# Dense product in native fp32 on 1104 columns, one-hots moved between ScalarE and VectorE, two dot pairs a unit on TensorE, top-k woven between dots

## The chip, the cores and the metric

The kernel runs on one core of one Trainium2 chip. Its time is the device time of one execution in microseconds (us). Three executions of the kernel before took 2683.0 to 2688.03 us, with a median of 2685.36 us.

## The reference, cut to what matters

One decoder layer on 272 tokens (16 meta, 256 real) of width 2048: a layer norm, two token mixers that read one input projection, a second layer norm, then a feed-forward part (PEER) that gathers experts, and a third norm. The change lies in the PEER part, for the 256 real tokens (two tiles of 128):

```
q = (t @ peer_wq).reshape(T, PEER_HEADS, 2, HALF_KEY)
sc = einsum('thpk,hpnk->thpn', q, peer_keys)
s_top, i_top = top_k(sc, 16)
cand = s_top[..., 0, :, None] + s_top[..., 1, None, :]
best_s, best_pos = top_k(cand, 16)           # 16 experts of 128*128 per token and head
g = softmax(best_s)
a = gelu(einsum('td,tkd->tk', xb, peer_u[eb]))
out = einsum('tk,tkd->td', g * a, peer_v[eb])  # 8 heads * 16 experts
```

Each token uses 128 of 16384 rows of peer_u and as many of peer_v, all 2048 wide, in fp32.

## The kernel before, in words

**Stages.** First the input projection and the mixers: weights stream in in 48 groups through SyncE's DMA queue, ScalarE and VectorE split each into two fp32r parts, TensorE multiplies. Then the **dots**, the **placement** and the **product**, which the change touches.

**Dots.** A unit is one head of one tile: 16 units (PH = 8 heads, 2 tiles), units 0 to 7 for tile 0 and 8 to 15 for tile 1. For a unit, `topk` on VectorE (17 chained steps) finds the 16 experts of each of 128 tokens, GpSimd issues 16 indirect DMAs (`gather_u`, L1852), each of which brings one row of peer_u per token (128 x 8 KB) into a ring of 8 buffers, and 16 dot products follow. VectorE makes most of them (`dot`, L1625, one instruction of 2048 columns each). From unit 2 on, the six rows of `PAIRS` (0,1), (5,6), (10,11) go to TensorE (`dots_pair`): it transposes the two rows block by block into PSUM (L817), ScalarE copies each of 8 blocks to `ut` (L908, `pair_copies`), TensorE multiplies with the transposed tokens (L430), and VectorE reads the diagonal (`pair_dots`, L1636). A buffer is free once its dot or its last transpose is done; GpSimd's queue waits for that in row order, so a row that is late holds back all gathers behind it. `gelu` and `softmax_exp` on ScalarE and `coefs` on VectorE give the weights.

**Placement.** The output is not summed from 256 gathered peer_v rows over all 2048 columns. For the first FD columns the kernel builds, per tile, a matrix of 128 tokens x 16384 experts that holds the weights (`wt0`, `wt1`): for each token, the product of two one-hot matrices (`oh`, 128 slots x 128 keys, one scaled by the weight). `one_hots` (L1654, L1655) makes them on VectorE in a ring of 5, `place` multiplies them on TensorE, `w_copy` moves four tokens at a time to SBUF on ScalarE. Tile 0 is placed during units 8 to 15, 16 tokens a unit, in pieces ahead of each `pair_dots` (`WTOK` = 6, 5, 5); tile 1 is placed after the last dot.

**Product.** 128 panels (128 experts x FD = 1344 columns of peer_v, 5376 B a row) stream in through SyncE's queue into 4 buffers. ScalarE and VectorE split each into an fp32r high and low part (`v_hi_of`, `v_lo_of`), and the matching piece of `wt` too (`w_hi_of`, `w_lo_of`). TensorE makes three fp32r products (high*high, high*low, low*high) for two tiles in three column cuts, 18 matmuls a panel, accumulated in six PSUM banks. The other 704 columns (2816 B a row) are gathered per slot (`gather_v`, L1863, ring of 4) and added by VectorE (`add_row`, L1681), 256 rows of 128 tokens. VectorE's order in this stage is add, split, add, split of `wt`. A last layer norm writes the output.

The order on each engine is written out by hand, and engines meet only at semaphores.

## Time and profile before

| | |
|---|---|
| median of 3 executions | 2685.36 us |
| the profiled execution | 2681.95 us |
| its span | 2680.1 us |
| busy: PE, DVE, ACT, POOL | 86%, 65%, 39%, 27% |
| granted TensorE clock, mean | 0.944 |
| HBM read | 655.69 MB, 245 GB/s over the span |

The page divides the span into 40 slices of 67 us. In slices 20 to 23 (1340 to 1608 us) the DMA share reads 9 (90% or more) and the rate is 380 to 395 GB/s; in the next six it reads 7 with 279 to 325 GB/s; slice 31 has 25 GB/s; after that it reads 8 or 9 with 284 to 323 GB/s. PE is TensorE, DVE VectorE, ACT ScalarE, POOL GpSimd, PEld TensorE's weight load.

### The profile page before, as it was taken

Reading aid. Unit: us, or ns where it says so; the run is one execution under the profiler, and the core shown is the slowest. Engines: PE = TensorE matmul, PEld = TensorE weight load, DVE = VectorE, ACT = ScalarE, POOL = GpSimd, SP = SyncE. Lnnn points to the kernel's source line nnn. Section 1 sums busy time; section 2 is a strip of 40 time slices with the busy share of each in tenths; the row PEclk is TensorE's granted clock in tenths of the full one; section 3 lists DMA queues with packets and bytes.
Section 4 is the critical chain, followed back from the end, with each engine's and each line's share of the span. In section 5 each row is a group of like instructions: output and inputs, shape, how many; then the busy total and the mean of one; then the engine's idle time right before and its main releaser. Section 6 shows DMA issues by size and latency. Waiting matters only on the chain.

```text
span 2680.1 us, 36941 instructions
## 1 busy us (share of the span) xinstructions
PE 2305.8 (86%) x13296; PEld 1992.0 (74%) x13296; DVE 1750.9 (65%) x2931; ACT 1035.3 (39%) x1481; POOL 717.5 (27%) x558
## 2 busy tenths in 40 slices
PE   7999999999999999993588877676778988888885
PEld 5888999988899888793466666565666777776774
DVE  5344455554455555578877777776759788878777
ACT  4444433444444444641233333333333333333331
POOL 0000000000000000023655533333330566556664
PEclk9999999999999999997798988888898999999997
DMA  6444555555555555395999987777760899889986
GB/s 174 115 140 141 172 177 185 185 177 192 193 177 190 188 188 177 109 371 230 395 383 393 380 324 304 306 307 279 311 258 25 284 314 323 309 307 316 311 314 221
DMA packets 217084, 659.68 MB, mean 246 GB/s; under 512 B 18784, under 2 KB 68064, under 8 KB 183520
## 3 DMA queue, kind: packets, MB, share of 16 engines
q0 software_dynamic: 57488, 361.79, 35.7%
q1 hardware_dynamic: 159456, 296.05, 33.2%
q8 instruction: 84, 1.38, 0.2%
q14 instruction: 56, 0.46, 0.0%
HBM read 655.69 MB, written 2.10 MB: 245 GB/s over the span
## 4 chain that ended last, share of the span: by engine, by line
PE 54%; DMA 20%; DVE 12%; issue 9%; ACT 2%; POOL 1%; DVEq 0%; POOLq 0%; SPq 0%; ACTq 0%
PE ps L430 50%; DMA v_rows<-in_v_gathered,idx_all 12%; DMA u_rows<-in_peer_u,idx_all 6%; DVE h L1681 3%; PE ps L817 3%; DVE junk L1625 2%; DMA v_raw<-in_peer_v 1%; DMA raw<-in_peer_wq 1%; POOL u_rows L1852 1%; ACT L908 0%; DVE lo L1289 0%; ACT hi L908 0%; POOL v_rows L1863 0%; PE ps L515 0%; ACT ut L908 0%
## 5 line engine op out<-in xcount | busy, mean ns | idle before, releaser
L1289 DVE TENSOR_TENSOR lo<-raw,hi 128x1024 fp32r<-128x1024 f32 x368 | 448.5, 1225 | 492.2 <-ACT hi L908 491.2
L908 ACT ACTIVATE hi<-raw 128x1024 fp32r<-128x1024 f32 x376 | 397.4, 1060 | 571.7 <-PE ps L430 560.1
L1852 POOL DMA_INDIRECT u_rows<-in_peer_u,idx_all x256 | 343.1, 1340 | 516.8 <-PE ps L817 335.8
L1625 DVE SCALAR_TENSOR_TENSOR junk<-u_rows,h 128x2048 bf16<-128x2048 f32 x172 | 388.6, 2288 | 122.0 <-DMA u_rows<-in_peer_u,idx_all 121.8
L430 PE MATMUL ps<-v_hi,w_hl 128*128 128x512 f32 (+1 forms) x1536 | 384.1, 379 | 77.2 <-DVE w_hl L1669 64.6
L430 PE MATMUL ps<-xh,hi 128*128 128x256 f32 (+2 forms) x1536 | 440.6, 287 | 2.5 <-ACT qkv L908 1.3
L1863 POOL DMA_INDIRECT v_rows<-in_v_gathered,idx_all x256 | 351.8, 1374 | 324.3 <-DVE h L1681 275.5
L430 PE MATMUL ps<-xh,lo 128*128 128x256 f32 (+2 forms) x1536 | 435.6, 284 | 0.0
L430 PE MATMUL ps<-xl,hi 128*128 128x256 f32 (+2 forms) x1536 | 434.9, 283 | 0.0
L430 PEld LDWEIGHTS ps<-v_hi,w_hl 128*128 128x128 f32 x1536 | 274.6, 194 | 144.9 <-issue 82.9
L430 PE MATMUL ps<-ut,h1t 128*128 128x256 f32 x1344 | 361.3, 398 | 19.4 <-ACT ut L908 19.3
L1681 DVE SCALAR_TENSOR_TENSOR h<-v_rows,coef_all,h 128x704 f32<-128x704 f32 x256 | 243.0, 949 | 116.5 <-DMA v_rows<-in_v_gathered,idx_all 114.4
L908 ACT ACTIVATE v_hi<-v_raw 128x1344 fp32r<-128x1344 f32 x128 | 170.1, 1329 | 366.1 <-DMA v_raw<-in_peer_v 324.3
L908 ACT ACTIVATE ut<-ps 128x512 f32<-128x512 f32 x336 | 197.3, 596 | 277.7 <-PE ps L817 277.7
L817 PE MATMUL ps<-ident,u_rows 128*128 128x128 f32 x1344 | 215.5, 293 | 101.4 <-DMA u_rows<-in_peer_u,idx_all 59.6
L430 PEld LDWEIGHTS ps<-xh,hi 128*128 128x128 f32 x1536 | 290.4, 189 | 12.3 <-issue 8.6
L430 PEld LDWEIGHTS ps<-xl,hi 128*128 128x128 f32 x1536 | 290.9, 189 | 0.0
L430 PEld LDWEIGHTS ps<-xh,lo 128*128 128x128 f32 x1536 | 290.1, 189 | 0.0
L817 PEld LDWEIGHTS ps<-ident,u_rows 128*128 128x128 f32 x1344 | 182.1, 153 | 135.1 <-issue 109.6
L430 PEld LDWEIGHTS ps<-ut,h1t 128*128 128x128 f32 x1344 | 237.9, 198 | 58.9 <-ACT ut L908 39.5
L1795 POOL TENSOR_TENSOR rstd<-rstd,m_half 128x1 f32<-128x1 f32 (+1 forms) x7 | 5.5, 786 | 816.0 <-DVE rstd L1530 800.4
L1663 DVE TENSOR_TENSOR v_lo<-v_raw,v_hi 128x1344 fp32r<-128x1344 f32 x128 | 198.6, 1552 | 17.2 <-ACT v_hi L908 17.2
(230 smaller groups left out, 3099.3 us busy)
## 6 DMA issues: line engine op xcount, KB each, us to landing
raw<-in_w_in SPq DMA_DIRECT2D x96, 1024.0 KB, 5.1
v_raw<-in_peer_v SPq DMA_DIRECT2D x128, 672.0 KB, 6.5
raw<-in_w_in SPq DMA_DIRECT2D x64, 256.0 KB, 3.1
raw<-in_w_in SPq DMA_DIRECT2D x32, 512.0 KB, 4.7
...
```

Source lines behind the costliest of these rows:

```text
L430: return nc.tensor.matmul(o, a, b, start=start, stop=stop)
L817: last = nc.tensor.transpose(ps[:, 3 + g % 2, (2 * n + r) * P:(2 * n + r + 1) * P], u_rows[k % RING][:, kt * P:(kt + 1) * P], ident[:, :])
L908: return nc.scalar.activation(o, i, f, **kw)
L1289: V.tensor_tensor(raw_lo[:, hh // 2, k4, :] if kept else lo[:, hh % SLOT_N, :, :], raw[:, hh // 2, k4, :], (kept_hi(hh) if kept else hi[:, ...
L1625: V.scalar_tensor_tensor(junk[:, n % 2, :], u_rows[k % (RING if u else HEAD_RING)][:, :], 1.0, h1[:, u // PH, :], ALU.mult, ALU.mult, accu ...
L1663: V.tensor_tensor(v_lo[i % RAWS][:, :], v_raw[i % RAWS][:, :], v_hi[i % HIS][:, :].bitcast(F32), ALU.subtract).then_inc(S("vlo_ready"), 1)
L1681: V.scalar_tensor_tensor(h1[:, T, FD:D], v_rows[n % VRING][:, :], coef_all[:, T, s:s + 1], h1[:, T, FD:D], ALU.mult, ALU.add).then_inc(S(" ...
L1795: Q.tensor_tensor(rstd[:cnt, n:n + 1], rstd[:cnt, n:n + 1], m_half[:cnt, 0:1], ALU.pow).then_inc(S(name + "_rstd"), 1)
L1852: Q.indirect_dma_start(u_rows[slot][:, :], None, peer_u, bass.IndirectOffsetOnAxis(ap=idx_all[:, n:n + 1], axis=0)).then_inc(u_in[slot], 16)
L1863: Q.indirect_dma_start(v_rows[n % VRING][:, :], None, v_gathered, bass.IndirectOffsetOnAxis(ap=idx_all[:, n:n + 1], axis=0)).then_inc(v_in ...
```

## The change

It changes five things (in the diff, the first `one_hots` is ScalarE's for tile 0, the second VectorE's for tile 1).

1. **Product.** FD is 1104, in three cuts of 368 columns. The panels (4416 B a row) and `wt` are multiplied as they are, in fp32, without the split: 6 matmuls a panel. The gathered part grows to 944 columns (3776 B a row). Five panel buffers in place of four, a ring of seven rows in place of four.
2. **Dots.** Two pairs a unit on TensorE, rows (0,1) and (8,9), so 12 dots a unit on VectorE in place of 10.
3. **Top-k.** A dot is put behind nearly each of the chained steps of `topk(u+2)`; before, the whole of `topk(u+2)` stood behind the dots of unit u. It reads the scores in place. `topk(1)` moves ahead of the dots of unit 0, between the splits of weight groups, and GpSimd's wait for the end of the projections moves behind the first four gathers of unit 1.
4. **Placement of tile 0.** The one-hots are made on ScalarE by Square, Relu(1 - x) and Copy with a scale, in chunks of four tokens (ring of 3 chunks), two chunks after each pair's copies; TensorE places a chunk half a unit later, behind the next pair.
5. **Placement of tile 1.** Still on VectorE after the last dot, in chunks: the key one-hots of four tokens by one instruction of 512 columns, every fourth chunk's key one-hots on ScalarE. The transpose of the slots stands ahead of `tile_open`.

```diff
-PAIRS = ((0, 1), (5, 6), (10, 11))
+PAIRS = ((0, 1), (8, 9))
-FD = 1344
+FD = 1104
+CW = 368
-RAWS, HIS, WBUFS = 4, 3, 2
-VRING = 4
+RAWS = 5
+VRING = 7
...
             def panel(i):
-                pe.wait_ge(S("vhi_ready"), i + 1)
-                pe.wait_ge(S("vlo_ready"), i + 1)
...
+                pe.wait_ge(vr_in[i % RAWS], 16 * (i // RAWS + 1))
                 for T in range(NT):
-                    for wn, v in ((0, v_hi[i % HIS]), (0, v_lo[i % RAWS]), (1, v_hi[i % HIS])):
-                        for n, (a, b) in enumerate(CUTS):
...
+                    for n, (a, b) in enumerate(CUTS):
+                        last = mm(ps[:, 3 * T + n, 0:CW], wt_rows(T, i, 1)[:, 0, :], v_raw[i % RAWS][:, a:b], False,
+                                  i == NKEY - 1)
...
+            def place(c):
+                bank = 6 + (c + 1) % 2
+                if c < CHUNKS_T:
+                    pe.wait_ge(S("oh_ready"), c + 1)
+                else:
+                    pe.wait_ge(S("oh_dve_ready"), c - CHUNKS_T + 1)
...
+            def one_hots(c):
+                if c >= OHR:
+                    act.wait_ge(S("w_done"), c - OHR + 1)
+                o = oh[c % OHR]
+                t0 = c % CHUNKS_T * WB
+                for q in range(WB):
+                    for n in range(2):
+                        ins = A(o[:, n, q, :], iota[:, :], ACT.Square, scale=-1.0, bias=slots_t[:, 1 + n, t0 + q:t0 + q + 1])
+                ins.then_inc(S("one_hot_squares"), 1)
+                act.wait_ge(S("one_hot_squares"), c + 1)
+                A(o[:, :, :, :], o[:, :, :, :], ACT.Relu, scale=-1.0, bias=one[:, 0:1]).then_inc(S("one_hot_units"), 1)
+                act.wait_ge(S("one_hot_units"), c + 1)
+                for q in range(WB):
+                    ins = A(o[:, 0, q, :], o[:, 0, q, :], ACT.Copy, scale=slots_t[:, 0, t0 + q:t0 + q + 1])
+                ins.then_inc(S("oh_ready"), 1)
...
                     pair_copies(u, pair)
+                    if pair == 0:
+                        gelu(u - 1)
+                        if u + 1 < 2 * PH:
+                            softmax_exp(u + 1)
                     if u >= PH:
+                        half = placed_half(u, pair)
+                        if half >= 0:
+                            for c in range(2):
+                                one_hots(2 * half + c)
+                        if half >= 1:
+                            for c in range(2):
+                                w_copy(2 * (half - 1) + c)
+            for c in range(2 * (2 * PH - 1), CHUNKS_T):
+                one_hots(c)
+            gelu(2 * PH - 1)
...
+            def one_hots(c):
+                dve.wait_ge(S("w_done"), c - OHR + 1)
...
+                if c % 4 != ACT_B:
+                    V.tensor_tensor(o[:, 1, :, :], iota[:, :].unsqueeze(1).to_broadcast([P, WB, P]),
+                                    slots_t[:, 2, t0:t0 + WB].unsqueeze(2).to_broadcast([P, WB, P]), ALU.is_equal)
+                for q in range(WB):
+                    ins = V.tensor_scalar(o[:, 0, q, :], iota[:, :], slots_t[:, 1, t0 + q:t0 + q + 1],
+                                          slots_t[:, 0, t0 + q:t0 + q + 1], ALU.is_equal, ALU.mult)
...
+            topk(1, scores_of(1), {4 * n - 10: lambda n=n: split_lo(G_WQ + 1, n) for n in range(AHEAD, 2 * AHEAD)})
...
+                    topk(u + 2, scores_of(u + 2), {n + 1: lambda n=n: unit_part(u, n) for n in range(min(parts, 15))})
...
-            for i in range(NKEY):
-                add_row(2 * i)
-                if i + 3 < NKEY:
-                    v_lo_of(i + 3)
-                add_row(2 * i + 1)
...
+            for n in range(NT * SLOTS):
+                add_row(n)
```

SyncE's first panel waits for the last top-k, the second and third for the last pair, the others for the last dot. GpSimd's `gather_v` waits for `tile_opened` at row 3 and for the last placement at row 5.

VectorE in unit 8, the first of tile 1, behind its first three dots. Before, one pair of `one_hots` per token stood ahead of the diagonal of a pair:

```order
L1625 SCALAR_TENSOR_TENSOR junk,dots<-u_rows_92,h_84 128x2048
L1659 TENSOR_SCALAR h_84<-h_84 128x704
L1654 TENSOR_SCALAR ohs<-iota,slots_t 128x128
L1655 TENSOR_SCALAR ohs<-iota,slots_t 128x128
...
L1636 SCALAR_TENSOR_TENSOR junk_148,dots<-ps,ident 128x128 x2
L1625 SCALAR_TENSOR_TENSOR junk,dots<-u_rows_95,h_84 128x2048
```

Now, in a later unit of tile 1 (unit 13), the steps of the top-k stand between dots, and no one-hot is left in a unit:

```order
L1582 MAX kv<-sc_all 128x8 x2
L1632 SCALAR_TENSOR_TENSOR junk,dots<-u_rows_90,h_84 128x2048
L1585 MAX_INDEX ki<-kv,sc_all 128x8
L1586 MATCH_REPLACE scw<-kv,sc_all 128x128
L1585 MAX_INDEX ki<-kv,sc_all 128x8
L1586 MATCH_REPLACE scw<-kv,sc_all 128x128
L1632 SCALAR_TENSOR_TENSOR junk,dots<-u_rows_91,h_84 128x2048
L1589 MAX kv<-scw 128x8 x2
L1632 SCALAR_TENSOR_TENSOR junk,dots<-u_rows_92,h_84 128x2048
```

The one-hots left VectorE's units, and each chained step now has a dot behind it.

ScalarE in tile 1 (`ut` is a pair's block, `wt` the placed weights). Before, a placed chunk was copied behind the copies of each pair:

```order
L908 ACTIVATE ut<-ps 128x512 x8
L908 ACTIVATE wt_103<-ps 128x128x4
L908 ACT_TABLE_LOAD
L908 ACTIVATE exps,exp_sums<-best,nbest 128x16
L908 ACTIVATE ut<-ps 128x512 x8
```

Now, first half of a unit:

```order
L904 ACTIVATE ut<-ps 128x512 x8
L904 ACT_TABLE_LOAD
L904 ACTIVATE gel<-dots 128x16
L904 ACT_TABLE_LOAD
L904 ACTIVATE exps,exp_sums<-best,nbest 128x16
L904 ACTIVATE ohs_101<-iota,slots_t 128x128 x8
L904 ACTIVATE ohs_101<-ohs_101,one 128x1024
L904 ACTIVATE ohs_101<-ohs_101,slots_t 128x128 x4
L904 ACTIVATE ohs_102<-iota,slots_t 128x128 x8
L904 ACTIVATE ohs_102<-ohs_102,one 128x1024
L904 ACTIVATE ohs_102<-ohs_102,slots_t 128x128 x4
L904 ACTIVATE wt_105<-ps 128x128x4 x2
```

26 one-hot instructions were put between a pair's copies and the next pair's; no table load stands among them.

TensorE in the product, one panel (`v_raw` is the panel as loaded), now:

```order
L428 MATMUL ps<-v_raw_109,wt_105 128x368 x3
L428 MATMUL ps<-v_raw_109,wt_0_106 128x368 x3
```

Six matmuls stand where 18 stood, and nothing of ScalarE or VectorE is ahead of them.

## Rows read from the trace of the kernel before

**Rows 1.** Windows by stage: us; PE, PEld, DVE, ACT, POOL busy; PEclk, DMA share, GB/s

```profile
1275.00:1539.00 264.00, 202.00 (x1088) 167.84 (x1088) 205.29 (x430) 98.54 (x169) 147.84 (x97) 0.89 0.97 387
1539.00:1980.00 441.00, 324.01 (x1775) 278.32 (x1775) 309.95 (x775) 152.75 (x259) 152.93 (x128) 0.87 0.78 306
2075.00:2660.00 585.00, 505.80 (x2304) 413.29 (x2304) 458.23 (x508) 204.52 (x251) 345.23 (x252) 0.97 0.88 305
```

**Rows 2.** Timeline of POOL: first gathers of units 1, 2, 8, and the last of unit 15

```profile
1244.45 0.94 POOL L1852 DMA_INDIRECT u_rows<-in_peer_u,idx_all  x1 [25.26 <-DVE idx_all L1614]
...
1275.60 1.91 POOL L1852 DMA_INDIRECT u_rows<-in_peer_u,idx_all  x1 [0.30 <-issue]
...
1539.24 0.94 POOL L1852 DMA_INDIRECT u_rows<-in_peer_u,idx_all  x1 [0.30 <-issue]
...
1979.62 0.93 POOL L1852 DMA_INDIRECT u_rows<-in_peer_u,idx_all  x1 [0.30 <-issue]
```

**Rows 3.** Groups by line and form from 1539 to 1980 us

```profile
L430 PE MATMUL ps<-ut,h1t 128*128 128x256 f32 x768 | 202.8, 392 | 16.8 <-ACT ut L908 16.8
L1625 DVE SCALAR_TENSOR_TENSOR junk<-u_rows,h 128x2048 bf16<-128x2048 f32 x80 | 180.5, 2288 | 70.1 <-DMA u_rows<-in_peer_u,idx_all 70.1
L1852 POOL DMA_INDIRECT u_rows<-in_peer_u,idx_all x128 | 153.5, 1199 | 288.1 <-PE ps L817 244.4 <-issue 43.4 <-DVE junk L1636 0.3
...
L430 PE MATMUL ps<-ohs 128*128 128x128 f32 x236 | 50.9, 383 | 91.5 <-DVE ohs L1655 91.4
```

**Rows 4.** Timeline of DVE: first and last of one top-k, its start and the dot behind

```profile
1421.80 0.29 DVE L1573 COPY sc<-sc_all 128x256 f32<-128x256 f32 x1
...
1433.33 2.29 DVE L1625 SCALAR_TENSOR_TENSOR junk<-u_rows,h 128x2048 bf16<-128x2048 f32 x1
```

**Rows 5.** Timeline of PE and ACT: a burst after a wait, one without, a pair's copies

```profile
1651.20 2.60 PE L430 MATMUL ps<-ohs 128*128 128x128 f32 x10 [8.58 <-DVE ohs L1655]
...
1665.08 1.28 PE L430 MATMUL ps<-ohs 128*128 128x128 f32 x10
...
1668.43 1.07 ACT L908 ACTIVATE ut<-ps 128x512 f32<-128x512 f32 x2
...
1677.17 0.60 ACT L908 ACTIVATE ut<-ps 128x512 f32<-128x512 f32 x1 [0.70 <-PE ps L817]
```

**Rows 6.** Groups of ACT by form, whole span

```profile
L908 ACT ACTIVATE hi<-raw 128x1024 fp32r<-128x1024 f32 x376 | 397.4, 1060 | 571.7 <-PE ps L430 560.1 <-DMA raw<-in_peer_wq 11.4
...
L908 ACT ACT_TABLE_LOAD x39 | 50.0, 1283 | 1.5 <-PEq L1892 0.8
...
L908 ACT ACTIVATE h<-ps,par 128x128 f32<-128x128 f32 x32 | 11.7, 467 | 0.1
...
L908 ACT ACTIVATE wt<-ps 128x128 f32<-128x128 f32 x32 | 8.7, 273 | 0.0
```

**Rows 7.** Timeline: last weights, first and last one-hot of tile 1, first panel

```profile
2002.62 0.23 DVE L1644 SCALAR_TENSOR_TENSOR coef_all<-gel,exp_scale,exps 128x16 f32<-128x16 f32 x1 [1.14 <-ACT gel L908]
...
2011.13 0.28 DVE L1654 TENSOR_SCALAR ohs<-iota,slots_t 128x128 f32<-128x128 f32 x1
...
2072.44 0.34 DVE L1655 TENSOR_SCALAR ohs<-iota,slots_t 128x128 f32<-128x128 f32 x1
...
2075.47 1.46 PE L430 MATMUL ps<-v_hi,w_hl 128*128 128x512 f32 x3 [2.15 <-ACT w_hl L908]
```

**Rows 8.** VectorE's tensor-tensor by form: 1024 columns (page), 256 columns (1539 to 1980 us)

```profile
L1289 DVE TENSOR_TENSOR lo<-raw,hi 128x1024 fp32r<-128x1024 f32 x368 | 448.5, 1225 | 492.2 <-ACT hi L908 491.2
...
L1604 DVE TENSOR_TENSOR oh_k<-pos2f,iota 128x256 f32<-128x256 f32 x14 | 5.3, 421 | 1.0
```

**Rows 9.** Product: `add_row` (2075 to 2660 us); timeline of PE at two panels' starts

```profile
L1681 DVE SCALAR_TENSOR_TENSOR h<-v_rows,coef_all,h 128x704 f32<-128x704 f32 x256 | 243.0, 949 | 116.5 <-DMA v_rows<-in_v_gathered,idx_all 114.4
...
2083.75 1.40 PE L430 MATMUL ps<-v_hi,w_hl 128*128 128x512 f32 x6
...
2087.47 1.40 PE L430 MATMUL ps<-v_hi,w_hl 128*128 128x512 f32 x6
```

274 lines of the change are left out of this document (115 added, 159 removed).

## The prediction

> **What bounds the kernel now.** I read the windows by stage first, then GpSimd's gathers in order of time, then the groups and the timelines of each stage.
>
> In the dots of tile 0 the DMA engines are the bound: share 0.97 at 387 GB/s, with 264 us from the first gather of unit 2 to that of unit 8 [rows 1, 2], (1539.24 - 1275.60) / 6 = 43.9 us a unit. In tile 1 the same 16 rows a unit take (1979.62 - 1539.24) / 8 = 55.0 us [rows 2] at a share of 0.78 [rows 1]. GpSimd waits there 244.4 us for a pair's last transpose, TensorE 91.4 us for VectorE's one-hots and VectorE 70.1 us for rows [rows 3]: a ring, in which one-hots on VectorE delay TensorE, which frees buffers late, which delays the rows that VectorE waits for. From the last weights to the first panel lie 2075.47 - 2002.62 = 72.9 us [rows 7]: VectorE makes one-hots. In the product the share is 0.88 at 305 GB/s for 585 us, with TensorE busy for 506 [rows 1]. It is nearly DMA-bound, with gaps in which neither queue has a row to move.
>
> **The change, part by part.** The sum is made against the profiled execution, 2681.95 us, which is 3.4 us under the median of the runs.
>
> *Start of the dots.* GpSimd sat 25.3 us before unit 1's first gather, for the top-k of unit 1 [rows 2]. That top-k now stands ahead of unit 0's dots. What comes next is late for VectorE: 16 dots of unit 1 and a top-k of 1433.33 - 1421.80 = 11.5 us [rows 4], 16 x 2.2 + 11.5 = 47 us, more than the 43.9 us that the rows need. So not 25 us are gained but what VectorE saves, and that is its own waits. Between 0 and 25 I take 10: the first rows are there early, but VectorE must still work off unit 1.
>
> *Tile 0, units 2 to 7.* VectorE gets two dots more and loses one pair's diagonals. In tile 1 it was busy 309.95 us in 8 units [rows 1], 38.7 each, of which 16 tokens of one-hots are 16 x 0.46 = 7.3 (from the run of 128: (2072.78 - 2011.13 - 3.1 for two splits) / 128 [rows 7]). The rest, 31.4, plus 2 x 2.29 [rows 3] is 36 us, and with the pauses of the chain at most 40, under 43.9. TensorE goes from three pairs to two. Rows 0, 1, 8 and 9 now all use the same two buffers: a pair holds them some 11 us, and new rows need about 8.5, so 19.5 to 21.5 against half a unit of 22. It fits barely, and I charge 0.3 us a unit, **+2** (between -3 and +15). The cover is the five rows that still stand in the ring; if a pair takes 2 us more it is gone, 6 x 4 = +24.
>
> *Tile 1, units 8 to 15.* VectorE is now as in tile 0. ScalarE takes the one-hots. Its costs: 8 blocks of a pair take 1677.77 - 1668.43 = 9.3 us once it is free [rows 5]. A small activation of 128 columns is 0.27 us without a per-partition operand, 0.47 with two, about 0.10 of it overlapped (11.7 us for 32) [rows 6]; I take 0.27 for one such operand. A chunk: 12 x 0.27 + 1.06 for 1024 columns + 0.3 for its two waits = 4.6 us. Half a unit: 9.3 + 2 x 4.6 + 2 x 0.55 for the copies of placed chunks = 19.6; once a unit, 2 x 1.28 for tables [rows 6] + 0.7 for gelu and exp; 42.5 us and two handovers of 0.5, **43.5 us**, the same as the DMA's 43.9. Nothing of it lies on VectorE's path. Three chains of 40 to 43.9 us that meet twice a unit don't run at the longest of them; I take 45.5 us: 8 x 45.5 = 364 against 440.4, **-76**. Bounds: 43.9 gives -89; with 0.37 for a small activation the chain is 48.5 and gives -52. On the engine choice, one token's one-hots cost 0.46 us on VectorE and 4.6 / 4 = 1.15 on ScalarE, worked out above. The Trainium skill, ScalarE: Activation LUTs, section Rules for kernel authors, says that relu and simple arithmetic belong on VectorE; by that rule, the work would be 2.5 times as long here and the placement would gain nothing. The rows say that ScalarE was busy 152.75 of 441 us [rows 1], so the longer work has room; the rule would put tile 1 at its present 440 us and the sum at 2649.
>
> *Last rows to last weights*, 23.0 us [rows 2, 7]: the last pair ends earlier in the unit, but two more chunks (9.2 us) stand ahead of the last gelu on ScalarE. **+2** (-3 to +12).
>
> *Tile 1's placement.* Before, 72.9 us. Now VectorE's chunk of four tokens: 512 columns of tensor-tensor, between 0.42 (256) and 1.23 (1024) [rows 8], by their slope 0.69, some 0.60 in a stream, and 4 x 0.26; 24 such chunks and 8 without the first: 24 x 1.64 + 8 x 1.04 = 48 us. TensorE: a matmul leaves two records, 8 records a chunk at 0.128 (10 in 1.28) [rows 5] are 1.0 us, hidden. Lead-in and last copy 9 us: 57, **-16** (-25 to 0).
>
> *Product.* TensorE: before, a panel of 18 took 2087.47 - 2083.75 = 3.72 us [rows 9]. Now 6 fp32 matmuls of 368 columns. `ut` x `h1t` is fp32 with 256 columns, two records each: 202.8 us busy for 384 matmuls [rows 3] is 0.53 us at a mean clock of 0.87 [rows 1], 0.46 at the full one, so 368 columns take 0.66 us and a panel 4.0: 128 x 4.0 = 508 us, a floor below what follows. VectorE: 256 adds of 944 columns at 949 + 240 x 1.04 = 1.20 us [rows 9] = 307 us, its splits gone. ScalarE nothing. DMA: before, 128 x 128 x 5376 + 256 x 128 x 2816 B = 180.4 MB, now 128 x 128 x 4416 + 256 x 128 x 3776 = 196.1 MB, less 5.2 MB that are in their buffers when the stage begins (5 panels, 5 rows). The rate is the term that no row shows. At this stage's 305 / 0.88 = 347 GB/s per full share and tile 0's share of 0.97 [rows 1], 336 GB/s and 568 us; at the unchanged 305 GB/s 626; at tile 0's 387 GB/s 493. I take 336: nothing holds the queues back any more (seven rows, add and product no longer in step), as in tile 0's ring, but rows stay of the size of this stage, about 4 KB against 8. With 7 us for start and last add 575: **-10** (-85 to +48). Layer norm and output have the same columns: 0.
>
> Sum: 2681.95 - 10 + 2 - 76 + 2 - 16 - 10 = 2574; with the median in mind **2575**.
>
> **The rivals.**
>
> *The product keeps its DMA rate* (0.15). For: no more than 0.88 was seen with two queues at once, and each row may cost more than its bytes. 190.9 MB at 305 GB/s + 7 = 633 us, +48, total 2575 + 58 = **2633** with no gain there. The Trainium skill, DMA: Bandwidth & Descriptors, section How a descriptor splits into AXI transactions, speaks for it: transfers go in pieces of 256 B from aligned addresses; 5376 and 2816 are multiples of 256, 4416 and 3776 aren't, and by my estimate from that page a gathered row costs 121 beats where its bytes make 118, 2.5% more. No row here shows an unaligned transfer. By that alone the product would take 14 us more, 2589. Against: ring depth was what stopped the gathers (add_row waited 114.4 us for rows [rows 9]).
>
> *ScalarE or the two shared buffers bound the units* (0.15). Units of 49 us in tile 1, 45.5 in tile 0: +28 + 8, **2611**. For: 43.5 is a sum of estimates, and a pair after a wait starts slow. Against: with three pairs tile 0 was at 0.97.
>
> *The product goes at tile 0's rate* (0.10): 493 us are under TensorE's 508, so 508 + 7 = 515 and **2515**. For: gathered rows of 3776 B are longer. Against: TensorE would then have to run without a gap.
>
> *Slower: TensorE's clock falls in the product* (0.05). It would wait 0.4 us in each panel of 4.4, and its granted clock is 2.4 GHz or half. Ten placement records took 2.60 us after a wait of 8.58 and 1.28 without [rows 5]. At half clock a panel is 8.0 us, all 128 make 1024 and the total **3024**. The point from which it decides: the total passes 2682 when the stage takes 682 us, 5.3 a panel, with a third of the columns at half clock. Against: the clock was 0.97 with TensorE idle 14% [rows 1], and now it would be 4.0 of 4.4, idle 10%.
>
> *The change doesn't take the one-hots off the path*: if ring and semaphores let TensorE wait for ScalarE as it did for VectorE, that is the second rival at its worst, 55 us a unit, 2651, inside its chance.
>
> **How the numbers follow.** The forecast, 2575, has 0.55. Together with the first two rivals it spans 2535 to 2633. The range reaches from **2525** to **2640** and leaves out the fast product and the slow clock, less than 2 in 10. Faster by more than 0.2% (5 us, about what a measurement of this kernel can tell from none): all but the slow clock and a pile-up of the bad ends, **0.95**; the same 0.01; slower 0.04.
>
> **What would show it.** GpSimd's first gathers of two units 44 us apart in tile 0 and 45 to 46 in tile 1, with a DMA share from 0.90 up; a ScalarE chunk of 4.6 us; under 60 us from the last weights to the first panel; in the product a share of 0.95 or more, a TensorE clock over 0.95, panels of 3.7 to 4.0 us with waits for `v_raw`. It is wrong if tile 1 stays above 50 us a unit, if the product takes over 600, or if TensorE, not the DMA, ends last there.

## The result and the profile after

| | before | after |
|---|---|---|
| median | 2686.49 us (4 runs) | 2497.56 us (4 runs) |
| ratio, with its 95% interval | | 0.9297 [0.9281, 0.9313] |
| the profiled execution | 2681.95 us | 2497.36 us |
| its span | 2680.1 us | 2495.5 us |
| HBM read | 655.69 MB | 671.42 MB |

The change makes the kernel 7.0% faster. The forecast was 2575 us, and the result lies 27 us under the lower end of its range, 2525. The two profiled executions differ by 184.6 us. Read against the marks that the prediction uses, the parts are:

| part | before | after | difference | predicted |
|---|---|---|---|---|
| first gather of unit 2 | 1275.60 | 1270.08 | -5.5 | -10 |
| tile 0, units 2 to 7 | 263.6 | 267.0 | +3.4 | +2 |
| tile 1, first to last gather | 440.4 | 370.6 | -69.8 | -76 |
| last gather to last weights | 23.0 | 31.7 | +8.7 | +2 |
| last weights to first panel | 72.9 | 58.8 | -14.1 | -16 |
| product, first panel to the end of the last | 584.5 | 477.2 | -107.4 | -10 |
| layer norm and output | 20 | 20 | 0 | 0 |

Six of seven terms came out within 7 us. The product alone brought ten times what was forecast for it.

The page of the changed kernel, its slices of 62 us. PEclk is TensorE's granted clock and DMA the share, both in tenths:

```profile
PEclk9999999999999999999967777777878899999998
DMA  5444465555565555547999999889998099999997
GB/s 163 130 143 143 135 193 179 185 182 188 185 196 183 186 188 190 172 149 255 354 357 366 376 385 381 347 347 356 353 375 331 17 374 411 412 411 411 409 410 294
```

The windows by stage of the changed kernel, with the columns of [rows 1]: tile 0, tile 1, product.

```profile
1270.00:1537.00 267.00, 155.42 (x765) 129.28 (x765) 226.44 (x432) 76.41 (x126) 178.54 (x96) 0.76 0.97 379
1537.00:1908.00 371.00, 230.45 (x1182) 196.14 (x1182) 271.59 (x494) 240.11 (x548) 191.49 (x128) 0.78 0.90 353
1998.00:2475.00 477.00, 474.98 (x1536) 291.65 (x1536) 304.58 (x255) 0.19 (x1) 383.99 (x251) 1.00 1.01 405
```

Against [rows 1]: tile 0 is as it was, tile 1 went from a share of 0.78 to 0.90, and the product from 305 to 405 GB/s. Six slices in a row (374 us) stand at 409 to 412 GB/s. TensorE is busy there for 474.98 of 477.00 us, so it is a bound. The DMA was expected to be the only one.

The groups of the same stage (1998 to 2475 us) say what each engine waited for (a group of matmuls has two records for each matmul):

```profile
L428 PE MATMUL ps<-v_raw,wt 128*128 128x368 f32 x1536 | 475.4, 472 | 2.6 <-DMA v_raw<-in_peer_v 1.8 <-ACT wt L904 0.8
L1859 POOL DMA_INDIRECT v_rows<-in_v_gathered,idx_all x251 | 384.0, 1530 | 129.0 <-issue 79.6 <-PE ps L428 43.5 <-DVE h L1680 5.9
L1680 DVE SCALAR_TENSOR_TENSOR h<-v_rows,coef_all,h 128x944 f32<-128x944 f32 x255 | 306.5, 1202 | 172.5 <-DMA v_rows<-in_v_gathered,idx_all 171.6
```

TensorE waits 1.8 us for panels in the whole stage. GpSimd, which issues the gathers, waits 5.9 us for a free row buffer. In 128 panels, 475.4 / 128 = 3.71 us each, a matmul of 368 columns is 0.62 us. VectorE waits 171.6 us for rows, and only the 5.9 us of GpSimd are waits for VectorE. The 18 fp32r matmuls of a panel before took 3.72 us [rows 9]: native fp32 on fewer columns made TensorE's panel no shorter, it took the splits away.

The end of the stage has a second chain that ends with TensorE's. The last matmuls and the last five adds of rows, from the timeline of 2455 to 2495.5 us:

```profile
2454.55 20.88 PE L428 MATMUL ps<-v_raw,wt 128*128 128x368 f32 x67
2469.60 6.46 DVE L1680 SCALAR_TENSOR_TENSOR h<-v_rows,coef_all,h 128x944 f32<-128x944 f32 x5 [0.81 <-DMA v_rows<-in_v_gathered,idx_all]
```

The matmuls end at 2475.43 and the adds at 2476.06. GpSimd's gathers stand back to back in this stage, 1.53 us and some 0.3 of issue each. So the stage is bound twice, by TensorE's matmuls and by the stream of gathered rows, and shortening one of them alone would gain almost nothing.

Tile 1 after the change, ScalarE's timeline through one unit (1730.05 to 1777.67 us):

```profile
1730.05 2.43 ACT L904 ACTIVATE ohs<-iota,slots_t 128x128 f32<-128x128 f32 x8
1732.51 1.15 ACT L904 ACTIVATE ohs<-ohs,one 128x1024 f32<-128x1024 f32 x1
1733.69 1.28 ACT L904 ACTIVATE ohs<-ohs,slots_t 128x128 f32<-128x128 f32 x4
1734.88 2.43 ACT L904 ACTIVATE ohs<-iota,slots_t 128x128 f32<-128x128 f32 x8
...
1739.70 1.05 ACT L904 ACTIVATE wt<-ps 128x512 f32<-128x512 f32 x2
1740.88 0.60 ACT L904 ACTIVATE ut<-ps 128x512 f32<-128x512 f32 x1
...
1751.21 0.60 ACT L904 ACTIVATE ut<-ps 128x512 f32<-128x512 f32 x1 [0.71 <-PE ps L815]
1751.83 1.28 ACT L904 ACT_TABLE_LOAD   x1
...
1754.96 2.43 ACT L904 ACTIVATE ohs<-iota,slots_t 128x128 f32<-128x128 f32 x8
...
1777.67 2.44 ACT L904 ACTIVATE ohs<-iota,slots_t 128x128 f32<-128x128 f32 x8
```

A chunk (the one-hots of four tokens) is 1734.88 - 1730.05 = 4.83 us, of which 2.43 are eight squares, 0.30 each. The eight copies of a pair take 1740.88 to 1751.81, 10.9 us, and in the other half 1765.56 to 1777.78, 12.2. Between them the engine has no idle time except the pair's own waits for transposes. The unit is 1777.67 - 1730.05 = 47.6 us, and the first gathers of units 9 and 15 are (1873.65 - 1588.82) / 6 = 47.5 us a unit apart (before, (1931.94 - 1590.93) / 6 = 56.8): the chain on ScalarE is the pace of tile 1.

The end of tile 1, ScalarE and VectorE of the changed kernel:

```profile
1918.90 2.43 ACT L904 ACTIVATE ohs<-iota,slots_t 128x128 f32<-128x128 f32 x8
...
1939.16 0.20 ACT L904 ACTIVATE gel<-dots 128x16 f32<-128x16 f32 x1
1939.39 0.23 DVE L1651 SCALAR_TENSOR_TENSOR coef_all<-gel,exp_scale,exps 128x16 f32<-128x16 f32 x1 [14.05 <-ACT gel L904]
```

After the last pair, four chunks stand ahead of the last gelu, 1939.16 - 1918.90 = 20.3 us. The last weights wait for it.

### The profile page after: what moved, and what is told of

It is laid out like the page before. It is cut to its first block, busy times and chain, and to the rows that moved or that the text cites. A ratio compares the mean times of both kernels' runs of the same rounds, so it can differ in the third digit from the quotient of the medians.

```text
span 2495.5 us, 32610 instructions
## 1 busy us (share of the span) xinstructions
PE 2122.0 (85%) x11632; PEld 1746.1 (70%) x11632; DVE 1571.4 (63%) x2299; ACT 927.9 (37%) x1571; POOL 837.0 (34%) x559
## 3 DMA queue, kind: packets, MB, share of 16 engines
HBM read 671.42 MB, written 2.10 MB: 270 GB/s over the span
## 4 chain that ended last, share of the span: by engine, by line
PE 58%; issue 15%; POOL 9%; DMA 7%; ACT 6%; DVE 5%; DVEq 0%; POOLq 0%; ACTq 0%
PE ps L428 52%; POOL v_rows L1859 7%; DMA u_rows<-in_peer_u,idx_all 6%; PE ps L815 5%; ACT ohs L904 3%; DMA v_rows<-in_v_gathered,idx_all 1%; POOL u_rows L1846 1%; DVE ohs L1665 1%; ACT L904 1%; DVE ohs L1662 0%; DVE lo L1296 0%; ACT hi L904 0%; PE ps L513 0%; ACT wt L904 0%; DVE h L1680 0%
## 5 line engine op out<-in xcount | busy, mean ns | idle before, releaser
L1846 POOL DMA_INDIRECT u_rows<-in_peer_u,idx_all x256 | 421.7, 1647 | 365.8 <-PE ps L815 199.7
L1632 DVE SCALAR_TENSOR_TENSOR junk<-u_rows,h 128x2048 bf16<-128x2048 f32 x200 | 458.2, 2292 | 136.8 <-DMA u_rows<-in_peer_u,idx_all 107.2
L428 PE MATMUL ps<-v_raw,wt 128*128 128x368 f32 x1536 | 475.4, 472 | 2.6 <-DMA v_raw<-in_peer_v 1.8
L428 PEld LDWEIGHTS ps<-v_raw,wt 128*128 128x128 f32 x1536 | 291.7, 190 | 186.0 <-DMA v_raw<-in_peer_v 2.6
L1680 DVE SCALAR_TENSOR_TENSOR h<-v_rows,coef_all,h 128x944 f32<-128x944 f32 x256 | 307.7, 1202 | 172.5 <-DMA v_rows<-in_v_gathered,idx_all 171.6
L428 PE MATMUL ps<-ut,h1t 128*128 128x256 f32 x896 | 267.7, 432 | 11.5 <-ACT ut L904 11.5
L904 ACT ACTIVATE ut<-ps 128x512 f32<-128x512 f32 x224 | 132.9, 597 | 343.2 <-PE ps L815 343.1
L428 PEld LDWEIGHTS ps<-ut,h1t 128*128 128x128 f32 x896 | 175.1, 218 | 42.3 <-ACT ut L904 25.5
L428 PE MATMUL ps<-hi,xh 128*128 128x512 f32 x256 | 101.7, 397 | 1.8 <-DVE t_y L1452 1.3
L428 PE MATMUL ps<-lo,xh 128*128 128x512 f32 x256 | 100.6, 393 | 0.0
```

The lines of the kernel that those rows point to most:

```text
L428: return nc.tensor.matmul(o, a, b, start=start, stop=stop)
L904: return nc.scalar.activation(o, i, f, **kw)
L1632: V.scalar_tensor_tensor(junk[:, n % 2, :], u_rows[k % (RING if u else HEAD_RING)][:, :], 1.0, h1[:, u // PH, :], ALU.mult, ALU.mult, accu ...
L1680: V.scalar_tensor_tensor(h1[:, T, FD:D], v_rows[n % VRING][:, :], coef_all[:, T, s:s + 1], h1[:, T, FD:D], ALU.mult, ALU.add).then_inc(S(" ...
L1846: Q.indirect_dma_start(u_rows[slot][:, :], None, peer_u, bass.IndirectOffsetOnAxis(ap=idx_all[:, n:n + 1], axis=0)).then_inc(u_in[slot], 16)
```

## The experiments

Two things needed an explanation: why the product's rate rose by a third, and what it was in the edits that shortened tile 1's middle units from 56.8 to 47.5 us. The first theory for the product was that the DMA engines carry more per unit of share when VectorE and ScalarE leave the splits out of their buffers' way (contention). The rivals were the rows' ring, from four to seven buffers, and the number of columns. For tile 1 the theory was ScalarE's chain, and the rivals were the half unit of delay and the third pair that TensorE lost. Each run is given by its ratio to the kernel before, measured beside it. That kernel's own median was between 2679.80 and 2686.49 us in these groups of runs, so two kernels of different groups that are less than 10 us apart are better compared by their ratios than by their medians.

### The product: what set its rate

**The columns alone**, in the kernel before:

```diff
-FD = 1344
+FD = 1104
+CW = 368
-CUTS = ((0, 512), (512, 1024), (1024, FD))
+CUTS = ((0, 368), (368, 736), (736, FD))
...
```

> The kernel before with only the column split changed to 1104 in three cuts of 368: panels still split into fp32r parts by ScalarE and VectorE, 18 matmuls a panel, rings of four. Theory A (the splits, not the columns, held the product back): VectorE's step for a panel is two adds of 1.20 us, one split of 1104 columns (about 1.3 us) and half of two splits of the weights (0.4), 4.1 us against 4.1 before, in step with rings of four; the DMA moves 1.53 MB a panel in place of 1.41, at the old 305 to 315 GB/s 4.9 us a panel, so the product takes 610 to 640 us and the kernel 2700 to 2740. Rival B (the columns did it): the product falls clearly under 585 us, toward 480 to 520, the kernel under 2620.

Measured: 2701.51 us, ratio 1.0094 [1.0066, 1.0122], so 0.9% longer. The product ran at 323 to 332 GB/s in the slices, where the kernel before has 307 to 323; the stage took 594 us, under the 610 to 640 expected. More columns on the row side raise the rate by a few per cent, far from 411 GB/s, and in sum they cost 22 us.

**More work on the engines that the change relieved**, in the changed kernel: a ScalarE copy of 1344 columns per panel in one run, a VectorE tensor-tensor of 768 columns per panel in the other. Nothing reads their output.

```diff
+            for i in range(NKEY):
+                act.wait_ge(S("panel_done"), i + 1)
...
+                A(scratch[:, :], wt0[:, 100:111, :].rearrange("p a b -> p (a b)")[:, 0:1344], ACT.Copy
+                  ).then_inc(S("scratch_done"), 1)
```

```diff
                 add_row(n)
+                if n % 2 == 0 and n:
...
+                    V.tensor_tensor(scratch[:, 0:768], wt0[:, 100:106, :].rearrange("p a b -> p (a b)"),
+                                    wt0[:, 106:112, :].rearrange("p a b -> p (a b)"), ALU.subtract
+                                    ).then_inc(S("scratch_done"), 1)
```

> The changed kernel, with one extra ScalarE copy of 128 x 1344 fp32 from one place of SBUF to another per panel, for which nobody waits: ScalarE's traffic of the kernel before, without its dependences. Theory D (ScalarE's traffic beside them stretches DMA packets, which took 20 to 25% more than their usual time before and 2% more now): DMA rate falls from 411 to some 350 GB/s, the product takes 540 to 570 us, kernel 2560 to 2590. Rival A (only dependences and order held the queues back): within 5 us of the changed kernel's 2497.6.

> The changed kernel, with one extra VectorE tensor-tensor of 128 x 768 fp32 per panel between the adds, for which nobody waits: about half of VectorE's splits of the kernel before. VectorE then needs 2 x 1.20 + 0.95 = 3.4 us a panel, under TensorE's 3.72. Theory D2 (VectorE's traffic stretches DMA packets or GpSimd's issues): product 510 us or more, kernel 2530 or more. Rival A (only order and dependences): under 10 us more than 2497.6.

Measured: 2498.31 us, ratio 0.9335 [0.9309, 0.9361], and 2503.57 us, 0.9347 [0.9325, 0.9369]. Windows of 2100 to 2400 us, first with the copies, then with the tensor-tensors:

```profile
2100.00:2400.00 300.00, 300.00 (x972) 184.30 (x970) 192.88 (x161) 107.23 (x81) 246.31 (x160) 1.00 1.02 411
```

```profile
2100.00:2400.00 300.00, 300.00 (x972) 184.31 (x971) 255.69 (x241) 0.00 (x0) 247.66 (x160) 1.00 1.02 411
```

ScalarE busy for 107 us, or VectorE for 256 instead of 193, and the rate stays at 411 GB/s. The contention theory falls for each load by itself: taking either off its engine was not what made transfers faster. Both loads at once, and VectorE's whole load of before, were not run. By their ratios the two kernels take 0.4% and 0.5% more than the change, and for the second the intervals don't overlap; its profiled execution is 4.0 us longer, and its last weights are already 4.0 us late (1943.40 for 1939.39), ahead of the first added instruction.

**Both rings as before, then each alone:**

```diff
-RAWS = 5
-VRING = 7
+RAWS = 4
+VRING = 4
```

> The changed kernel with four panel buffers and four row buffers in place of five and seven. Theory A (the splits held the queues back, not the rings): a row has 1.86 us, a slot of four 7.4 us, and its cycle is issue 1.3, transfer and landing about 4 to 5, add 1.2: about 7, so the product goes from 477 to 480 to 500 us, kernel 2500 to 2520. Rival C (ring depth was what stopped the gathers before): the product goes back to 550 us or more, kernel 2570 or more.

> The changed kernel with the ring of gathered rows at four, panel buffers at five as changed. Theory C (too few gathers in flight cost the DMA engines their rate; the four-and-four kernel took 88 us more): all of that loss is here, product about 565 us, kernel 2575 to 2595. Rival C2 (the panel buffers share it): 2530 to 2560.

> The changed kernel with four panel buffers, the ring of rows at seven as changed. Theory C: nothing, within 5 us of 2497.6, since TensorE waits for a panel only 2 us in all. Rival C2: 20 us or more above it.

| panels | rows | median | ratio |
|---|---|---|---|
| 4 | 4 | 2585.53 us | 0.9646 [0.9622, 0.9669] |
| 5 | 4 | 2586.28 us | 0.9626 [0.9608, 0.9643] |
| 4 | 7 | 2503.69 us | 0.9319 [0.9303, 0.9335] |
| 5 | 7 | 2497.56 us | 0.9297 [0.9281, 0.9313] |

With four row buffers 88 us of the gain are gone: theory C, and not A's 2500 to 2520. The fifth panel buffer is worth some 6 us, where theory C said 5 at most, and the intervals overlap. This is where most of the product's 107 us came from: three more buffers for the gathered rows. The rest is small: with four of them, the changed kernel's product takes 2570.18 - 1998.55 = 571.6 us against the 584.5 of before.

Windows with four row buffers (five panels), while TensorE has panels and after its last:

```profile
2000.00:2475.00 475.00, 473.94 (x1533) 290.70 (x1531) 244.64 (x204) 0.00 (x0) 249.28 (x205) 1.00 0.97 359
```

```profile
2475.00:2570.00 95.00, 0.02 (x1) 0.00 (x0) 59.38 (x50) 0.00 (x0) 61.92 (x47) 0.52 0.78 244
```

TensorE does its 128 panels in 475 us here too. In that time VectorE adds 204 of the 256 rows, 475 / 204 = 2.33 us each, and the rest takes 95 us with TensorE idle. Without panels beside them, the same four buffers bring 50 rows in these 95 us, 1.90 each: a buffer's turn (from one gather into it to the next) falls from 9.3 to 7.6 us, so it isn't a constant of the ring. In these 475 us the share is 0.97. A reader of that number alone would call it DMA-bound, as I read tile 0's; but the same 475 us carry 407 GB/s in the changed kernel, with more buffers.

**How many row buffers:**

> The changed kernel with five row buffers in the product (four gave 2586, seven 2498). Theory A (each buffer is busy 9.3 us a turn, whatever their number: 4 x 2.33 us a row in the run with four): a row each 9.3 / 5 = 1.86 us, which is TensorE's own pace of 3.72 / 2, so five buffers already nearly reach the full rate: 2498 to 2506 us and 405 GB/s or more. Theory B (more transfers in flight share the queues, and a buffer's turn grows to 10 us or more, as 4 x 2.26 became 5 x 2.01 in the kernel before): a row each 2.0 us, 256 rows in 515 us: about 2535 us, and 385 GB/s.

> Six row buffers. Theory A: as with seven, 2495 to 2502 us. Theory B: a turn of 10.5 to 11 us over six is 1.8 us a row, under TensorE's 1.86, so here too the time of seven: 2496 to 2506 us. A third, that each buffer is worth the same down to seven: (2586 - 2498) / 3 = 29 us each, so 2527.

Windows of 2100 to 2400 us with four, five and six row buffers (three kernels; the changed one has 411 GB/s there):

```profile
2100.00:2400.00 300.00, 300.00 (x972) 184.35 (x971) 154.94 (x129) 0.00 (x0) 163.50 (x129) 1.00 0.97 359
```

```profile
2100.00:2400.00 300.00, 300.00 (x972) 184.39 (x971) 179.14 (x149) 0.00 (x0) 211.37 (x150) 1.00 1.01 393
```

```profile
2100.00:2400.00 300.00, 300.00 (x972) 184.52 (x971) 190.71 (x159) 0.00 (x0) 248.28 (x159) 1.00 1.02 408
```

| row buffers | us per row | buffer's turn | median | ratio |
|---|---|---|---|---|
| 4 | 300 / 129 = 2.33 | 9.3 us | 2586.28 us | 0.9626 [0.9608, 0.9643] |
| 5 | 300 / 150 = 2.00 | 10.0 us | 2519.52 us | 0.9389 [0.9363, 0.9415] |
| 6 | 300 / 159 = 1.89 | 11.3 us | 2499.36 us | 0.9329 [0.9307, 0.9350] |
| 7 | 300 / 160 = 1.88 | 13.1 us | 2497.56 us | 0.9297 [0.9281, 0.9313] |

Beside panels, a buffer's turn (gather, landing, add) is 9 to 10 us when the ring is the limit, and longer where it isn't. From six buffers on a row takes 1.88 us, and GpSimd waits at most 0.3 us of these 300 for a buffer: the ring is no longer the limit. Against 1.88, a turn of 10.0 us wants 10.0 / 1.88 = 5.3 buffers, so five are short, six are enough, and the seventh buys at most a few us.

What holds a row at 1.88 us is not TensorE, though its half panel takes nearly the same, 3.71 / 2 = 1.86: in the changed kernel neither a gather nor an `add_row` waits for a matmul. The run with 1344 columns on TensorE, told below, has rows of 2816 B that come faster than half a panel of 2.25 us. It gathers its last row at 2362.51, some 210 us before its last matmul ends. While rows come, its rate is nearly that of the change (window of 2010 to 2360 us):

```profile
2010.00:2360.00 350.00, 350.00 (x933) 176.96 (x932) 226.53 (x238) 0.00 (x0) 271.39 (x239) 1.00 1.01 398
```

A row takes 350 / 238 = 1.47 us there. A gather's time on GpSimd is no fixed price either. With four, five and seven row buffers it is 1.27 us at 359 GB/s, 1.42 at 393 and 1.55 at 411 (2100 to 2400 us), with rows of 2816 B 1.14 at 398, and the shortest take 0.94. Queues that are full near 400 to 411 GB/s would look like this; no run separates the DMA engines from GpSimd's issuing. So the changed product meets two limits at once, and that they lie within 1 us of each other is luck.

For five, theory A (a fixed turn) said 2498 to 2506 and theory B 2535: the measured 2519.52 lies between, since the turn grew from 9.3 to 10.0 us. For six, both said about what was measured, and "each buffer is worth the same" (2527) is out.

**One more row buffer in the kernel before:**

```diff
-VRING = 4
+VRING = 5
```

> The kernel before with a ring of five gathered rows in place of four, nothing else changed. Theory C (ring depth held its product at 305 GB/s): a row's cycle of 8.9 us over five slots is 1.8 us, so its product is bound next by VectorE's 3.9 to 4.1 us a panel and falls from 585 to 525 to 545, kernel 2635 to 2645. Rival A (VectorE's and ScalarE's splits in step with the adds held it): within 10 us of the kernel before.

Measured: 2625.76 us, ratio 0.9777 [0.9760, 0.9793]. One buffer gives 60 us, with splits and columns as they were, 9 us better than the range of theory C, and its product takes 525 us. Waits of 2100 to 2400 us (engine, line, what it waited for: us in total, times, longest), of the kernel before:

```profile
POOL v_rows L1863 <- DVE h L1681: 108.8, 99, 3.2
DVE h L1681 <- DMA v_rows<-in_v_gathered,idx_all: 58.4, 53, 2.5
```

with five row buffers:

```profile
POOL v_rows L1865 <- DVE h L1681: 58.5, 86, 2.6
DVE h L1681 <- DMA v_rows<-in_v_gathered,idx_all: 29.0, 43, 1.9
```

and of the changed kernel:

```profile
DVE h L1680 <- DMA v_rows<-in_v_gathered,idx_all: 108.0, 161, 1.1
POOL v_rows L1859 <- DVE h L1680: 0.3, 1, 0.3
```

In the kernel before, both sides of the row ring waited for each other, GpSimd for a buffer that VectorE had to free and VectorE for the row. VectorE's order also bound the two halves of the product together: `add_row(2i)`, the split of a panel, `add_row(2i + 1)`. So a panel could not go faster than two rows, and 585 us / 256 = 2.29 us a row, 9.1 a turn, was the pace of everything. The change cut that tie and deepened the ring; now the wait for a buffer is 0.3 us. Cutting the tie alone left a row at 2.33 us, as the run with four row buffers shows. Whether the splits would have let the kernel before reach the same time with six or seven is open: no run has them there, and at five its TensorE is already busy for 280.56 of 300 us.

**TensorE as a new bound**, the changed kernel with 1344 columns on TensorE again (buffers are moved to make room, and the third and fifth panels wait longer):

```diff
-FD = 1104
-CW = 368
+FD = 1344
...
+CW = 448
...
```

> The changed kernel with the old column split: 1344 columns in three cuts of 448 in native fp32, 704 gathered, rings of five and seven. TensorE is the bound: 6 x 448 columns at 1.69 ns (0.62 us for 368) are 4.53 us a panel, 128 of them 580 us against 475; kernel 2595 to 2605, with the DMA share near 0.85 and 311 GB/s. Rival (something else than TensorE would pace it, as in the kernel before): above 2620.

Measured: 2597.94 us, ratio 0.9676 [0.9658, 0.9694], 100 us over the change. The time is as expected; the share is not: it was to be near 0.85, and is 1.01 while the rows come, since they run ahead. Group of 2100 to 2400 us:

```profile
L430 PE MATMUL ps<-v_raw,wt 128*128 128x448 f32 x800 | 300.8, 539 | 0.0
```

800 records are 400 matmuls, 0.75 us each, against 0.62 for 368 columns (972 records in 300 us): both some 1.68 ns a column at a granted clock of 1.00, which is four cycles of 2.4 GHz. 128 panels of 4.5 us are 576 us. So 1104 columns are no detail: with native fp32, TensorE's time goes with the columns, and the split between TensorE and the rows is what the change had to shift.

### Tile 1: what set the unit

**Less work on ScalarE.** This kernel leaves out the Relu and three of four Copies of each chunk, so tile 0's weights are not placed rightly; it only shows what their time is worth:

```diff
-                A(o[:, :, :, :], o[:, :, :, :], ACT.Relu, scale=-1.0, bias=one[:, 0:1]).then_inc(S("one_hot_units"), 1)
-                act.wait_ge(S("one_hot_units"), c + 1)
-                for q in range(WB):
-                    ins = A(o[:, 0, q, :], o[:, 0, q, :], ACT.Copy, scale=slots_t[:, 0, t0 + q:t0 + q + 1])
-                ins.then_inc(S("oh_ready"), 1)
+                A(o[:, 0, 0, :], o[:, 0, 0, :], ACT.Copy, scale=slots_t[:, 0, t0:t0 + 1]).then_inc(S("oh_ready"), 1)
```

> The changed kernel, whose ScalarE makes only the Squares of tile 0's one-hots and one small Copy a chunk; Relu and three Copies a chunk are left out, so the weights of tile 0 are not placed rightly. Theory E (ScalarE's chain of copies and one-hots, 47.6 us a unit back to back, is what paces tile 1): 2.1 us less a chunk, 8.5 us a unit, so the units fall from 47.7 to the DMA's 44 and the last gelu comes 4 us earlier; with three chunks' worth less behind the last pair 2497.6 falls by 26 to 35, to 2463 to 2472. Rival F (the two buffers that both pairs share pace the units): they stay at 46.5 or more, kernel above 2485.

Measured: 2474.35 us, ratio 0.9234 [0.9210, 0.9258]. The gathers of units 9 to 15 are 44.3 us apart on average ((1855.97 - 1590.08) / 6), where they were 47.5. ScalarE's length was the pace, as theory E has it, and under it lies the 44 us of tile 0. The total is 2 us over the range that this theory gave.

**The one-hots of tile 0 on VectorE**, all of them, a half, and the last two chunks only. Everything else stays as in the change, with the placing half a unit later:

```diff
...
                 elif n == 6:
                     pair_dots(u, 0)
+                    tile0_chunks(u, 0)
                 elif n == 13:
                     pair_dots(u, 1)
+                    tile0_chunks(u, 1)
...
```

> The changed kernel with tile 0's one-hots made on VectorE in chunks of four tokens (one instruction for the keys, four for the scaled ones, 1.63 us a chunk) behind each pair's diagonal, still placed half a unit later. If only the move to ScalarE gained in tile 1, the units go back toward 55 us (kernel 2550 or more). Theory E: VectorE has 34 us of work a unit and gets 6.5 more, 40.5 plus its pauses, ScalarE falls to 30: units of 44 to 45.5 and a last gelu right behind the last pair, 2465 to 2485, faster than with ScalarE.

> The changed kernel with every odd chunk of tile 0 and chunk 30 on VectorE, the other even ones on ScalarE. ScalarE 9.6 us less a unit, 38, VectorE 3.3 more, 37: no engine near the DMA's 44 us, so the units are DMA-bound: 44.3 against 47.7, 7.5 x 3.4 = 25 and 9 at the end: 2460 to 2470, the fastest of these. Rival: the shared buffers hold the units at 46 or more, 2478 or more.

> The changed kernel with only the last two of tile 0's 32 chunks on VectorE, which waits there 14 us for the last gelu. Two chunks of 4.8 us go from ScalarE's path between the last pair and the last gelu: 8 to 10 us less, 2488 to 2490. Rival: TensorE or the copies of placed chunks are next, 3 us or less gained.

| on VectorE | median | ratio |
|---|---|---|
| chunks 0 to 31 | 2471.52 us | 0.9212 [0.9186, 0.9238] |
| every other, and chunk 30 | 2469.89 us | 0.9212 [0.9189, 0.9235] |
| chunks 30 and 31 | 2488.31 us | 0.9277 [0.9256, 0.9298] |
| none (the change) | 2497.56 us | 0.9297 [0.9281, 0.9313] |

Both upper rows beat the change, by 26 and 28 us. Windows of 1589 to 1812 us, of the change and with all chunks on VectorE:

```profile
1589.00:1812.00 223.00, 141.76 (x731) 121.00 (x730) 168.22 (x334) 159.50 (x370) 118.36 (x78) 0.79 0.90 354
```

```profile
1589.00:1812.00 223.00, 146.21 (x781) 125.68 (x780) 203.62 (x441) 72.74 (x122) 138.04 (x80) 0.80 0.96 369
```

VectorE is busy 203.62 of 223 us and still not in the way: the units are (1860.13 - 1588.72) / 6 = 45.2 us apart and the DMA share is 0.96. So moving the one-hots to ScalarE didn't bring the gain of tile 1; it cost a part of it. The last two chunks alone bring 9 us by the medians and 5 by the ratios, whose intervals overlap. In the profile the last gelu starts 1932.24 - 1921.63 = 10.6 us after the last pair, where it was 20.3.

**Without the half unit of delay**: TensorE places a chunk right behind the pair in whose half it is made. One run with the one-hots on VectorE, one with them on ScalarE:

```diff
-                    if u >= PH and placed_half(u, pair) >= 1:
+                    if u >= PH and placed_half(u, pair) >= 0:
                         for c in range(2):
-                            place(2 * (placed_half(u, pair) - 1) + c)
-            for c in range(2 * (2 * PH - 2), CHUNKS_T):
+                            place(2 * placed_half(u, pair) + c)
+            for c in range(2 * (2 * PH - 1), CHUNKS_T):
```

> One-hots of tile 0 on VectorE as in the run that took 2471.5 us, but TensorE places them in the half unit in which they are made, right behind the pair, as the kernel before did. Theory A (the half unit of delay is what took the one-hots off the path): TensorE waits in each half for the pair's diagonals and 3.6 us of one-hots, 4 to 5 us, twice a unit, and the units of tile 1 grow from 44.7 to 48 to 53 us: total 2500 to 2540. Theory B (the delay is worth little; the third pair and VectorE's load were what made 55 us): TensorE is idle 77 us of 223 in these units, the wait falls into that, and units stay at 45 to 46: total 2468 to 2482, a few us of it from a shorter end of tile 1.

> The changed kernel with its one-hots on ScalarE, but placed in the half unit in which they are made. ScalarE makes the two chunks behind the pair's copies, in 9.7 us, and TensorE waits for them before it turns the next pair. Theory A (without the delay the one-hots on ScalarE are a chain in series with TensorE): a half unit is a pair of 11 us, two chunks of 9.7, the placing and the next wait; units from 47.6 to 52 or more, total 2530 to 2580. Theory B (ScalarE's own chain of 47.6 us sets the pace in either order): 2490 to 2505.

| one-hots on | placed | median | ratio | unit |
|---|---|---|---|---|
| VectorE | half a unit later | 2471.52 us | 0.9212 [0.9186, 0.9238] | 45.2 us |
| VectorE | at once | 2492.97 us | 0.9293 [0.9271, 0.9316] | 48.7 us |
| ScalarE | half a unit later | 2497.56 us | 0.9297 [0.9281, 0.9313] | 47.5 us |
| ScalarE | at once | 2527.66 us | 0.9435 [0.9411, 0.9459] | 51.0 us |

TensorE's row in the groups of 1589 to 1812 us, one-hots on VectorE, with the delay and without it:

```profile
L436 PE MATMUL ps<-ohs 128*128 128x128 f32 x144 | 17.5, 275 | 0.0
```

```profile
L436 PE MATMUL ps<-ohs 128*128 128x128 f32 x144 | 34.1, 432 | 81.9 <-DVE ohs L1679 81.9
```

The delay takes 81.9 us of waits in five units out of TensorE's way, and with them the slow start: the same 144 records take 17.5 us after other work and 34.1 after a wait. It is worth 3.5 us a unit with the one-hots on either engine. With them on VectorE theory B had expected nothing and A 3 to 8, and the total, 2492.97, lies between their ranges. With them on ScalarE both ranges were missed as well: A said 52 us a unit or more and 2530 to 2580, against 51.0 and 2527.66. But 48.7 is still 8.1 us under the 56.8 of before. That remainder belongs to what both runs share with the change: two pairs in place of three, one-hots in chunks behind the pair's diagonals and no longer ahead of them, and the top-k between the dots. No run here takes these apart.

## Why the prediction was wrong

**Product, the step that failed.** The prediction put the rate as "this stage's 305 / 0.88 = 347 GB/s per full share" times a share of 0.97, 336 GB/s. It took GB/s per share to be a property of this stage's transfers, with only the share left to win. The runs showed that the rate per share rises with the rows in flight: 359 / 0.97 = 370 with four row buffers in the changed kernel, 393 / 1.01 = 389 with five, 411 / 1.02 = 403 with seven. The kernel before has the same: 347 / 0.95 = 365 GB/s with five row buffers. The right sum starts from the buffer's turn: 9.1 us / 4 = 2.29 us a row before, and 10 us / 7 = 1.4 us after. By that, the ring of seven could not bind; next came TensorE's floor and the rate at which the queues themselves top out, which only the runs showed: 190.9 MB at 411 GB/s are 465 us, under that floor. The forecast would have been the floor, the third rival. The ring's depth was in the prediction, but only to argue for the share. The prediction's sign of being wrong, that TensorE and not the DMA ends last, came out as a tie: the last add ends 0.6 us behind the last matmul.

**Product, a second step.** The floor of 508 us for TensorE came from 0.66 us a matmul, scaled from a group at a mean clock of 0.87 [rows 1, 3]. It is 0.62, and 508 - 475 = 33 us of the floor were not there. Dividing by a mean clock did not give the duration at full clock: the group mixes bursts after waits with bursts in a stream. At the 1.68 ns a column measured here, 256 columns are 0.43 us and not the 0.46 of the prediction.

**The third rival had the right mechanism**: 387 GB/s or more and TensorE as the bound without a gap, 0.10, 2515 us. I held against it that TensorE would have to run without a gap; it did, 474.98 of 477.00 us. With the matmul at 0.62 it would have given 475 + 7 = 482 us for the stage and 2482. That the rows kept up to within 1 us was no part of it.

**The first rival** (rate unchanged) is out, and no price of unaligned rows shows: per full share the kernel before has 313 / 0.91 = 344 GB/s from 2100 to 2400 us with 5376 and 2816 B, and 325 / 0.92 = 353 with 4416 and 3776 B (the columns alone). The section How a descriptor splits into AXI transactions of the Trainium skill's DMA: Bandwidth & Descriptors gave, by my estimate, 2.5% more beats for a gathered row; no run shows them in the time. The same page's section Where 436 GB/s comes from says that for transfers between HBM and SBUF the HBM side binds, at some 358 GB/s for a core. This kernel runs on one core; the 411 GB/s of its stage are over that, and the measurement decides.

**Start of the dots**: -5.5 for -10, inside its bounds, for the reason given: VectorE still had dots to work off. The first gather of unit 1 comes 22 us earlier (1222.28 for 1244.45), but up to unit 2's first GpSimd waits 14.1 us for dots, where it waited 3.4.

**Tile 0**: +3.4 for +2. At 267.0 / 6 = 44.5 us a unit the two shared buffers hold as predicted.

**Tile 1**: 370.6 / 8 = 46.3 us a unit for 45.5, but the mean hides three parts. Unit 8 takes 51.7 us from its first gather to unit 9's, as before; the six units behind it take 47.5 each, where they took 56.8; and the last gather of unit 15 comes 34.0 us after its first (47.7 before). The middle units are 2 us over the forecast, and the short last one brings the mean back near it by luck. The chain was right in kind, but longer than the 43.5 us summed. Its terms: chunk 4.83 for 4.6 (a square issues every 0.30 us, not 0.27), 4 x 0.23 = 0.9 us a unit; copies of a pair 10.9 and 12.2 for 9.3, 4.5 us a unit. The second grew with TensorE's clock: the granted clock of tile 0 was 0.89 before [rows 1] and 0.76 now, with TensorE busy 155 of 267 us, and in tile 1 0.78 for 0.87. With fewer pairs it idles more (6.64 and 7.73 us ahead of the two pairs of this unit), and the start of each pair runs at half clock, as the windows of 1739.7 to 1745 and 1764 to 1772 us show (last figures: clock, DMA share, GB/s):

```profile
1739.70:1745.00 5.30, 5.24 (x19) 4.46 (x20) 1.74 (x1) 2.75 (x6) 2.12 (x3) 0.52 1.00 414
1764.00:1772.00 8.00, 6.24 (x21) 4.81 (x20) 6.10 (x12) 3.51 (x9) 3.84 (x3) 0.50 1.00 380
```

The blocks behind them come every 1.30 us in both kernels, so the extra time of the copies lies in these starts. The two handovers of 0.5 are inside these copies, so 43.5 + 0.9 + 4.5 - 1.0 = 47.9 is the measured 47.6. The 2 us that were added to the chain for three chains that meet weren't there: it ran by itself at its own length, and the two errors cancelled in part. The second rival had the mechanism, ScalarE as the bound, with 49 us a unit.

**ScalarE or VectorE**: by the rule of the Trainium skill, ScalarE: Activation LUTs, section Rules for kernel authors, this arithmetic belongs on VectorE. I set the slack of ScalarE against it. The rule's choice is faster by 2497.56 - 2471.52 = 26 us. What I had tied to it, that without the move the placement would gain nothing (2649 us), is wrong: with the delay, VectorE's one-hots gain more than ScalarE's. The idea that ScalarE's slack makes the longer work free failed, since that work became tile 1's pace.

**Last weights**: +8.7 for +2. Two chunks were counted ahead of the last gelu, four stood there, 9.7 us more. With two of them on VectorE the last weights come 1935.99 - 1910.48 = 25.5 us after the last gather instead of 31.7.

**Placement of tile 1**: -14.1 for -16. VectorE's chunk took 1.63 us (1947.58 to 1949.21), predicted 1.64.

**The chance of faster** (0.95) was right. The slow-clock rival did not come near: clock 1.00 in the product, where TensorE hardly waited. The range left out the fast product by design, and that was the case that came.
